# Down projections by square blocks, with seven block products in four of eleven super-groups

## The reference, cut to what matters

```
h = rms_norm(x, g)
u = dwconv3(h @ w_up)                # 2048 -> 2 * 5632, taps over tokens
gate, up = split(u)
y = (act(gate) * up) @ w_down        # 5632 -> 2048: "down"; act is gelu, then silu
x = x + rms_norm(y, g_post)
```

## Time and profile before

| | us |
|---|---|
| median of 3 runs | 2511.09 |
| lowest, highest | 2509.42, 2518.72 |
| span of the profiled execution | 2510.2 |
| PE busy | 2496.8 |
| DVE, ACT, POOL busy | 1656.4, 1336.6, 221.3 |
| bytes moved by DMA | 462.25 MB, mean 184 GB/s |

### The profile page before, as it was taken

The page is one execution under the profiler, slowest core; times in us unless marked ns, Lnnn a source line. Parts: engine busy times, 40 slices in busy tenths (PEclk is TensorE's granted clock), DMA queues, the critical chain, the costliest instruction groups (busy, mean ns, idle before and its releaser), DMA issues.

```text
span 2510.2 us, 40508 instructions
## 1 busy us (share of the span) xinstructions
PE 2496.8 (99%) x15417; PEld 2153.2 (86%) x15417; DVE 1656.4 (66%) x2020; ACT 1336.6 (53%) x1754; POOL 221.3 (9%) x96
## 2 busy tenths in 40 slices
PE   9999999999999999999999999999999999999998
PEld 9999988888888888888888888888888888888887
DVE  6665675776777775445495968775677777775444
ACT  6554564656565554445545455454656556554343
POOL 1000000031211211000000000000012131221000
PEclk9999999999999999999999999999999999999999
DMA  7865445566666666555655655545566666666554
GB/s 236 254 206 154 118 140 185 180 190 188 189 186 191 192 188 210 195 194 187 193 173 164 176 154 174 160 149 188 174 186 192 191 186 191 188 189 211 194 194 156
DMA packets 241720, 462.25 MB, mean 184 GB/s; under 512 B 14392, under 2 KB 23921, under 8 KB 240961
## 3 DMA queue, kind: packets, MB, share of 16 engines
q1 hardware_dynamic: 239937, 453.45, 58.9%
q0 software_dynamic: 1568, 7.10, 0.9%
q10 hardware_dynamic: 96, 0.02, 0.0%
HBM read 458.40 MB, written 2.12 MB: 183 GB/s over the span
## 4 chain that ended last, share of the span: by engine, by line
PE 98%; ACT 0%; DMA 0%; DVE 0%; issue 0%; SPq 0%; DVEq 0%; ACTq 0%
PE acc L232 13%; PE acc L252 13%; PE acc L233 13%; PE acc L234 13%; PE tp L252 13%; PE tp L254 7%; PE acc L254 7%; PE acc L967 2%; PE acc L969 2%; PE acc L970 2%; PE acc L1193 1%; PE acc L1195 1%; PE acc L1194 1%; PE tp L1696 1%; PE acc L975 1%; PE acc L977 1%
## 5 line engine op out<-in xcount | busy, mean ns | idle before, releaser
L219 DVE TENSOR_TENSOR wlo<-raw,whi 128x1024 fp32r<-128x1024 f32 x855 | 1073.8, 1263 | 725.9 <-ACT whi L214 724.3
L214 ACT ACTIVATE whi<-raw 128x1024 fp32r<-128x1024 f32 x855 | 902.5, 1059 | 991.1 <-PE acc L234 458.2
L252 PE MATMUL acc<-ahl,whi 128*128 128x512 f32 x1408 | 490.2, 392 | 0.6 <-DVE ahl L337 0.6
L252 PE MATMUL tp<-ahl,whi 128*128 128x512 f32 x1408 | 489.5, 391 | 0.0
L254 PE MATMUL tp<-ahl,wlo 128*128 128x256 f32 x1408 | 394.2, 280 | 0.0
L254 PE MATMUL acc<-ahl,wlo 128*128 128x256 f32 x1408 | 394.1, 280 | 0.0
L252 PEld LDWEIGHTS acc<-ahl,whi 128*128 128x128 f32 x1408 | 263.4, 187 | 59.0 <-issue 1.0
L252 PEld LDWEIGHTS tp<-ahl,whi 128*128 128x128 f32 x1408 | 263.3, 187 | 57.7
L232 PE MATMUL acc<-whi,ahl 128*128 128x512 f32 x752 | 298.7, 397 | 1.8 <-DVE ahl L1794 1.5
L234 PE MATMUL acc<-whi,ahl 128*128 128x512 f32 x752 | 293.0, 390 | 0.0
L233 PE MATMUL acc<-wlo,ahl 128*128 128x512 f32 x752 | 292.7, 389 | 0.0
(11 more groups left out here) (286 smaller groups left out, 2963.8 us busy)
## 6 DMA issues: line engine op xcount, KB each, us to landing
raw<-in_w_up_dram SPq DMA_DIRECT2D x176, 512.0 KB, 4.1
raw<-in_ffn_w_in_dram SPq DMA_DIRECT2D x176, 512.0 KB, 4.2
raw<-in_hgrn_w_in_dram SPq DMA_DIRECT2D x160, 512.0 KB, 3.6
raw<-in_w_down_dram SPq DMA_DIRECT2D x88, 512.0 KB, 3.9
raw<-in_ffn_w_out_dram SPq DMA_DIRECT2D x88, 512.0 KB, 3.7
raw<-in_w_in_dram SPq DMA_DIRECT2D x87, 512.0 KB, 4.1
raw<-in_w_out_dram SPq DMA_DIRECT2D x32, 512.0 KB, 3.6
raw<-in_hgrn_w_out_dram SPq DMA_DIRECT2D x32, 512.0 KB, 3.8
```

The source lines that it names most:

```text
L214: act.activation(whi[:, s, :], raw[:, s, :], ACT.Copy).then_inc(hi_done, 1)
L219: dve.tensor_tensor(wlo[:, s, :], raw[:, s, :], whi[:, s, :].bitcast(F32), ALU.subtract).then_inc(lo_done, 1)
L252: pe.matmul(o[:, ct % 2, :].rearrange("p (a t) -> p a t", a=2), whi[:, s, c], ahl[:, :, kt, :], start=(kt == 0), stop=False, skip_group_ch ...
```

## The change

**Square blocks.** Down now takes one super-group at a time for a pair of column groups, so that 512 hidden features by 1024 columns form four chunks, in blocks (rows half r, column group c). Both accumulators fill side by side. The super-groups go in the order `DOWN_ORDER` = 0, 1, 2, 3, 5, 4, 6, 10, 7, 9, 8, once for each of the two pairs.

**Seven products.** For the super-groups in `S_SGS` = 2, 5, 9, 10 the 2x2 block product is formed with seven block products instead of eight (Winograd's form of Strassen's scheme). Each of the seven multiplies one of seven left parts (128 tokens by 256 rows, rounded and remainder) by one of seven right parts and takes 6 matmuls. Three right parts are raw chunks, four are sums that DVE adds in place in `raw` (`weight_sums`), so such a super-group has seven round-and-remainder steps for its four loads. Product sums are held in PSUM, three of them in the two `tp` banks' quarters, over all four such super-groups of a pair, and DVE combines them with eight 128x512 operations (`sum_11` to `sum_22`) while PE does the last, ordinary super-group (`down_last`), whose four blocks each wait for one of these results (`pre_sums`).

**Left parts.** POOL makes the seven left parts (`seven_parts`, nine instructions in place of two, with `cvu` as scratch). For super-groups 2 and 5 that is inside up; 9 is only multiplied there (into `hraw`), and 10 and then 9 are split after up has ended (`down_pool`).

**Ends.** The norm's gain row is loaded in two halves. At the end of down the third column group is squared and scaled token half by token half before the fourth is done (`c1_act`, `c1_y`), the sum of squares is finished per half (`down_rest`), and in down2 `last_y` of the second half stands ahead of the reciprocal. `back_load` waits, by the table FREED, until the last product that reads a buffer has its remainder.

The core of the diff:

```diff
+S_RAW = (0, 2, 3, 0, 1, 2, 3)
+S_A = (0, 6, 1, 4, 3, 5, 2)
+S_SGS = (2, 5, 9, 10)
+LATE = (10, 9)
+DOWN_ORDER = (0, 1, 2, 3, 5, 4, 6, 10, 7, 9, 8)
...
+FREED = {d.m: d.n for d in DOWN}
...
+                if m < RING:
+                    sp.wait_ge(lo_done, cb[ph] - RING + m + 1)
+                else:
+                    sp.wait_ge(lo_done, cb[ph] + FREED[m - RING] + 1)
...
+        def one_of_seven(pe, ph, d):
+
+            out = (P1B, cols(ph, 1)[:, 0, :], cols(ph, 0)[:, 0, :], P5B, P7B, P6B, cols(ph, 0)[:, 1, :])[d.j]
...
+            for kk in range(CK):
+                w = slice(kk * GC, (kk + 1) * GC)
+                xh, xl = part7(d.sg, 0, a, kk), part7(d.sg, 1, a, kk)
+                pe.matmul(out, xh, whi[:, d.n % RING, w], start=fresh and kk == 0, stop=False, skip_group_check=True)
+                pe.matmul(out, xh, wlo[:, d.n % RING, w], start=False, stop=False, skip_group_check=True)
+                mm = pe.matmul(out, xl, whi[:, d.n % RING, w], start=False, stop=False, skip_group_check=True)
+            mm.then_inc(chunk_used, 1)
...
+        def down_last(pe, ph, i, n, sg, nxt):
+
+            for b, (t, c) in enumerate(blocks_of(i, nxt)):
+                pe.wait_ge(sem("pre_sums"), 4 * (NPAIR * DOWNS.index(ph) + i) + b + 1)
...
+                if d.i and d.sg == DOWN_ORDER[0] and d.j in (0, 2):
+                    group(pe, gb[ph] + 2 * d.i + RC[d.j][1])
...
+                if d.sg in LATE and d.i == 0 and d.j == 0:
+                    pe.wait_ge(ready, FG + 1 + LATE.index(d.sg))
...
+        def down_hi(act, ph, d):
+
+            n = cb[ph] + d.n
+            if d.summed and d.j >= 3:
+                act.wait_ge(sem("sums"), ub[ph] + SUMS[d.i, d.sg] + d.j - 2)
+            else:
+                act.wait_ge(landed[d.m % RING], 16 * ((rb[ph] + d.m) // RING + 1))
+            act.wait_ge(chunk_used, n - RING + 1)
...
+            if d.j == 0:
+                dve.wait_ge(landed[1], 16 * ((rb[ph] + d.m + 1) // RING + 1))
+                add(0, 1)
+            if d.j == 1:
+                add(1, 2)
+            if d.j == 2:
+                dve.wait_ge(sem("sums"), s0 + 1)
+                add(2, 0)
+                dve.wait_ge(sem("sums"), s0 + 3)
+                add(3, 2)
...
             for i in range(FG - 1):
...
+                if i in LATE:
+                    hidden_product(pool, ph, i, hraw, sem(f"{ph}_hid"))
+                    continue
+                hidden_product(pool, ph, i, cvg, sem(f"{ph}_pr"))
...
+                if i in S_SGS:
+                    seven_parts(pool, ph, i, cvg, hsum[S_SGS.index(i)])
+                else:
+                    two_parts(pool, ph, i)
```

More of the change, by code:

```diff
@@ L49, with __init__, down_steps @@
 HGRP = 5
+RC = ((0, 0), (1, 0), (0, 1), (1, 1))
+SC = ((0, 0), (0, 1), (1, 1), (1, 0))
+S_RAW = (0, 2, 3, 0, 1, 2, 3)
+S_A = (0, 6, 1, 4, 3, 5, 2)
+S_SGS = (2, 5, 9, 10)
+LATE = (10, 9)
+S_MADE = tuple(sg for sg in S_SGS if sg not in LATE) + LATE
+R_SGS = tuple(sg for sg in range(FG) if sg not in S_SGS)
+DOWN_ORDER = (0, 1, 2, 3, 5, 4, 6, 10, 7, 9, 8)
+NPAIR = D // (2 * GC)
+DOWNS = ("down1", "down2")
+REST = {"out1": 0, "down1": 2, "out2": 6, "down2": 8}
+class Step:
+    def __init__(self, n, i, sg, j, m, last):
+        self.n, self.i, self.sg, self.j, self.m, self.last = n, i, sg, j, m, last
+        self.summed = sg in S_SGS
+def down_steps():
+    steps = []
+    for i in range(NPAIR):
+        for p, sg in enumerate(DOWN_ORDER):
+            m0 = 4 * (i * FG + p)
+            for j in range(7 if sg in S_SGS else 4):
+                steps.append(Step(len(steps), i, sg, j, m0 + (S_RAW[j] if sg in S_SGS else j), p == FG - 1))
+    return steps
+DOWN = down_steps()
+N_DOWN = len(DOWN)
+M_DOWN = 4 * FG * NPAIR
+DOWN_FIRST_SUM = next(d.n for d in DOWN if d.summed)
+assert DOWN_ORDER[0] in R_SGS and DOWN_ORDER[1] in R_SGS and DOWN_ORDER[-1] in R_SGS and DOWN_ORDER[-2] in S_SGS
+FREED = {d.m: d.n for d in DOWN}
+PAIR_END = [max(d.n for d in DOWN if d.i == i) + 1 for i in range(NPAIR)]
+SUM_END = [max(d.n for d in DOWN if d.i == i and d.summed) + 1 for i in range(NPAIR)]
+SUMS = {}
+for d in DOWN:
+    if d.summed and d.j == 0:
+        SUMS[d.i, d.sg] = 4 * len(SUMS)
+N_SUMS = 4 * len(SUMS)
 T_KC, T_VC, T_DQ, T_DK, T_NQ, T_KS, T_KW = 0, 2, 4, 12, 20, 28, 30
@@ L88, in bass_two_blocks @@
             ybuf = sb("ybuf", [P, NT, D], where=r)
-            hhi = sb("hhi", [P, FT, S], F32R, r)
-            hlo = sb("hlo", [P, FT, S], F32R, r)
+            hhi = sb("hhi", [P, 4 * len(R_SGS), S], F32R, r)
+            hlo = sb("hlo", [P, 4 * len(R_SGS), S], F32R, r)
+            hsum = [sb(f"hsum{j}", [P, 2, 14, P], F32R, r) for j in range(len(S_SGS) - len(LATE))]
+            hraw = sb("hraw", [P, 4, S], where=r)
         with ExitStack() as r:
@@ L178, in bass_two_blocks @@
         with ExitStack() as r:
-            gbd = sb("gbd", [P, D], where=r)
+            hlate = [sb(f"hlate{j}", [P, 2, 14, P], F32R, r) for j in range(len(LATE))]
+            gbd = sb("gbd", [P, 2 * GC], where=r)
         acc = [ctx.enter_context(nc.psum_tensor(f"acc{i}", [P, NT, GC], F32)) for i in range(2)]
@@ new lines, in bass_two_blocks, with blocks_of, part7, regular @@
+        BY_TOKEN = ((0, 0), (0, 1), (1, 0), (1, 1))
+        BY_COLUMNS = ((0, 0), (1, 0), (0, 1), (1, 1))
+        def blocks_of(i, nxt):
+            return BY_TOKEN if i == NPAIR - 1 and not nxt else BY_COLUMNS
+        def part7(sg, lo, a, kk):
+            h = hlate[LATE.index(sg)] if sg in LATE else hsum[S_SGS.index(sg)]
+            return h[:, lo, 2 * a + kk, :]
+        def regular(pe, ph, d):
+            r, c = RC[d.j]
+            for kk in range(CK):
+                kt, w = 4 * R_SGS.index(d.sg) + CK * r + kk, slice(kk * GC, (kk + 1) * GC)
+                first = d.sg == DOWN_ORDER[0] and r == 0 and kk == 0
+                for t in range(NT):
+                    xh, xl = hhi[:, kt, t * P:(t + 1) * P], hlo[:, kt, t * P:(t + 1) * P]
+                    pe.matmul(cols(ph, c)[:, t, :], xh, whi[:, d.n % RING, w], start=first, stop=False, skip_group_check=True)
+                    pe.matmul(cols(ph, c)[:, t, :], xh, wlo[:, d.n % RING, w], start=False, stop=False, skip_group_check=True)
+                    mm = pe.matmul(cols(ph, c)[:, t, :], xl, whi[:, d.n % RING, w], start=False, stop=False,
+                                   skip_group_check=True)
+            mm.then_inc(chunk_used, 1)
@@ L2091, in _ @@
             up_load(sp, "up1", T["w_up"][0])
-            back_load(sp, "down1", T["w_down"][0], DCH)
+            back_load(sp, "down1", T["w_down"][0])
             m2_load(sp)
@@ L2136, in _ @@
             up_act(act, "up1", 0, sem("out1_x"), 8)
-            back_act(act, "down1", 1, DCH, "in2")
+            back_act(act, "down1", 1, "in2")
             m2_act(act)
             up_act(act, "up2", 1, sem("out2_x"), 8)
-            back_act(act, "down2", 3, DCH, None)
+            back_act(act, "down2", 3, None)
         @block.vector
```

334 lines of the change are left out of this document (249 added, 85 removed).

## The result

The changed kernel takes 2568.03 us (median of 4 runs, 2566.55 to 2569.93), the kernel before 2514.9 us (2509.42 to 2519.96). The ratio is 1.0216, with a 95% interval of 1.0195 to 1.0238. The prediction said 2521, from 2500 to 2538, and "within 0.5%" as the likeliest case. The forecast was wrong in size: it had 0.4% more time, the runs show 2.2% more, above the whole range. The profiled spans are 2510.2 and 2567.0 us, so 56.8 us have to be found.

The account below looks back on a forecast made before the run. It took TensorE (98% of the chain) as the bound: 2510.2 - 21.8 + 9.8 + 11.0 + 8 + 4 - 0.5 = 2520.7 us of span, plus 0.9 to the runs' median, given as 2521 us, range 2500 to 2538.

Parts of the forecast that it names:

- within 0.5%: Whole kernel: the forecast case, 2521 us, with changes under 0.5% (12.6 us) counted as no change; chance 42%.
- Matmuls removed: TensorE in both down phases: 504 matmuls per pair in place of 528, 96 fewer in all, -21.8 us.
- Down's stalls by the walk: Down1 and down2: TensorE's waits, found by stepping through loads, remainders and additions by the code's waits; +9.8 and +11.0 us.
- the spacing of the landings: Down's loads: 3.6 us for one alone, 1.7 us between landings in a burst, with 1.5 and 2.0 as range.
- loads too slow in a burst: Rival, four loads behind each seven-product group: 2.0 us between landings, 39 us of stalls, time 2539 us; chance 15%.
- The clock: TensorE: short waits lowering the clock is seen nowhere in the trace; no separate price or chance.
- GpSimd against VectorE: Start of each down: GpSimd's late splitting holds up VectorE, 4 us a phase between bounds 0 and 6.5; +8 us.
- strict exclusion: Rival: GpSimd and VectorE fully exclude each other; down 6.5 us each, up 2.8 at four places, 2533 us; chance 23%.
- Up: Up phases: GpSimd's longer work on super-groups 2 and 5 loses 1.0 us at each of four places, +4 us.
- The ends: Program's end and start of in2: last_y moves out of VectorE's chain, about -0.3 us, in2 about as much; -0.5 us.
- Sum: Whole kernel: 2510.2 - 21.8 + 9.8 + 11.0 + 8 + 4 - 0.5 = 2520.7 us of span, given as 2521 us.
- Slower: Whole kernel: the outcome of a time more than 0.5% longer than before; chance 38%.

Follow-up runs that it names:

- e3_nolate: New kernel without GpSimd's late splitting of super-groups 10 and 9 in down; TensorE reads the parts of 2 and 5 instead. Span 2556.3 us, ratio 1.0164.
- e6_two: New kernel with two seven-product super-groups (2 and 9) in place of four, each behind two or more ordinary ones. Span 2533.2 us, ratio 1.0104.
- e2_halfload: New kernel with each load of down cut to its first 128 rows, 256 KB in place of 512 KB. Span 2535.2 us, ratio 1.0102.
- e1_noadds: New kernel without the four additions that make the sums of weights in each seven-product super-group. Span 2519.5 us, ratio 1.0052.
- The probes: Two versions of the kernel before with unused VectorE additions, so that TensorE waits at chosen places. Spans 2535.3 and 2521.3 us, ratios 1.01 and 1.0074.
- e8_endfix: New kernel with the last column group's two squares at the end of down2 written to PSUM nobody reads any more. Ratio 1.0223.
- e12_better: New kernel with the fourth addition behind the fourth remainder and down2's last squares written to free PSUM. Median 2554.51 us, ratio 1.0176.
- e11_nolate_half: New kernel with both half the bytes for each load of down and no late splitting on GpSimd in down. One execution, span 2518.1 us.

## Why the prediction was wrong, step by step

**Matmuls removed**, -21.8: right. 1056 in the new order take 239.40 us, and each phase has 48 fewer.

**Down's stalls by the walk**, +9.8 (its five parts add up to 9.7) and +11.0. Down without the late splitting lost 23.4 and 23.2 us (e3_nolate, 251.9 and 251.7 less 228.5), so this is the largest miss, 26 us. The places were right: fourth products of 5 and 9, next chunk, pair ends; none behind two ordinary groups (e6_two). The sizes were not. Of the 46.6 us, 8.1 were lost at the lower clock and 4.2 to GpSimd's product at super-group 2, which the walk left out. Some 34 remain for the walk's 20.8.

The step that failed here is the spacing of the landings: I took 1.7 us in a burst. Four loads issued at 1155.3, 1156.5, 1157.6 and 1158.8 landed 3.9, 5.2, 5.9 and 6.0 us later, so 2.5, 1.8 and 1.3 us apart. Over eight loads behind a seven-product group, from first landing to last, the walk had 11.9 us (7.1 to 19.0) and e3_nolate shows a median of 13.3, or 1.9 us each. The walk itself gave 20.8 us for 1.7 and 39 for 2.0; for 1.9 that makes about 33, an estimate, against the 34. So the mechanism was right and this size was off. The rival "loads too slow in a burst" put the switch at 1.75 and had 15%. That the bytes matter is shown by e2_halfload. That they matter only together with the additions is shown by e1_noadds, where eight landings took as long (12.5 to 15.0 us) and the fourth products waited nowhere. The fourth product of 9 waited 2.0 us where the walk had 1.0:

```profile
1171.25 1.06 ACT L636 ACTIVATE whi<-raw 128x1024 fp32r<-128x1024 f32 x1 [4.10 <-DMA raw<-in_w_down_dram]
...
1175.75 2.48 DVE L649 TENSOR_TENSOR raw<-raw 128x1024 f32<-128x1024 f32 x2
1178.15 4.62 DVE L641 TENSOR_TENSOR wlo<-raw,whi 128x1024 fp32r<-128x1024 f32 x4
...
1179.42 0.50 PE L568 MATMUL tp<-whi,hlate 128*128 128x512 f32 x1 [1.87 <-DVE wlo L641]
```

A load sets ScalarE's start, the remainders and additions stand in a row behind it, and PE waits for the fourth remainder.

**The clock.** I wrote that short waits lower it nowhere in the trace, which was so, since the trace had no waits, and put no price on it. That is the second step that failed. In the new kernel the stretches at a granted clock of 0.50 cost 7.0 and 6.3 us in the downs, 13 us in all, and in e3_nolate 4.9 and 3.2. The probes show that waits alone bring it: 1.7 us more behind 2.94 us, nothing behind 1.81.

**GpSimd against VectorE**, +8: measured 18.1 (8.8 and 9.3). The waits themselves grew by 6.2 and 6.0 us, close to the strict case's 6.5 a phase, and the rest is nearly all lower clock (2.1 and 3.1 us more than in e3_nolate). So the price of strict exclusion was right for down. The step that failed is the choice of 4 in its place.

**Up**, +4: measured +9.8 in the profiled executions. The waits were sized about right, one of 1.05 us in up1 and two of about 1.1 in up2, not the strict case's 2.8 at four places. What I could not have from the trace is the slower pace behind a wait, 6 us of up1's 7.3.

**The ends**, -0.5: measured +4.2. `last_act` of the first half waits for the last sum, and the scaling of the third column group and more row sums came into VectorE's last 10 us. I costed what moved away and not what moved in.

**Sum.** -21.8 + 46.6 + 18.1 + 9.8 + 4.2 = 56.9. In down the rivals "loads too slow in a burst" and "strict exclusion" were both true at once. I had them as alternatives, each added to the forecast alone. Their prices for down together give 2521 + 18 + 5 = 2544, already out of the range. The 13 us at the lower clock, the 6 more in up and the 5 more at the ends bring it to 2568. (The price of 18 for the loads is met in part by luck, since GpSimd's product makes up 4 of it.) Slower had 38%, less than the 42% of "within 0.5%".

## What to carry to other kernels

A scheme that saves matmuls but makes the feeding uneven is paid from the lead of the ring: with four buffers the loads behind a heavy group come as a burst, and one neighbour of slack does not win it back. Halving bytes, leaving out an engine's work, and both together separate such causes cheaply. When a kernel that never waits starts to wait, price the wait, what the clock may do behind waits of some 2 us and more, and all bad cases at once.

## What the runs showed of the hardware that I had not expected

**Pace of the turned matmuls in up.** With a granted clock of 1.00 the loop of 512-wide and 256-wide matmuls runs in one of three forms: 391 and 280 ns, 393 to 394 and 277 (as fast), or 399 and 281 (1.9% slower, 8.6 us over a whole up phase). It changes at a wait of PE and then holds for hundreds of us, to the next wait or the end of the phase. At the first wait of 1.05 to 1.07 us in up1 the new kernel and five variants went to the slow form. e8_endfix did not, and e12_better only at its second wait. In e3_nolate up1, and in e11_nolate_half up2, ran slowly from the start, with no wait but the 0.28 us one that every kernel has there. What decides the form was not found. It may be why runs of the kernel before lie anywhere from 2509 to 2522 us; no trace of such a run was taken.

**GpSimd and VectorE taking turns.** A GpSimd instruction on 256 numbers took 1.71 us behind a VectorE operation and 0.73 ahead of one, while VectorE's operation beside it grew from 1.23 to 1.75 us. A GpSimd product that came while VectorE's operations followed each other without a pause took 8.92 us (956.79 in e3_nolate), in place of 4.45 in the kernel before.

**The lower clock behind a wait**, 0.50 granted, cost 1.7 to 2.9 us where it came behind a single wait. Whether it came differed between waits of the same length (1.9 us, 3.1 us). What decides it no run here shows.
